# Sums over partitions with a matrix of ones: one fp32 product against two float32r products of split operands

## What is computed

```
def l2norm(x):
    return x * lax.rsqrt(jnp.sum(x * x, axis=-1, keepdims=True) + EPS)
...
q = l2norm(q.reshape(bsz, s, GDN_HEADS, GDN_DK).astype(f32)) * (GDN_DK ** -0.5)
k = l2norm(k.reshape(bsz, s, GDN_HEADS, GDN_DK).astype(f32))
g = -jnp.exp(gdn_a_log.astype(f32)) * jax.nn.softplus(gdn_a.astype(f32) + gdn_dt_bias.astype(f32))
...
gcum = jnp.cumsum(heads_to_chunks(g), axis=-1)
```

## Time and profile before

| | |
|---|---|
| median of 3 runs | 2578.36 us (2577.38 to 2578.86) |
| span of the profiled execution | 2574.7 us |
| TensorE (PE) busy | 2549.0 us, 99% |
| VectorE (DVE) busy | 1367.1 us, 53% |
| ScalarE (ACT) busy | 1237.7 us, 48% |
| GpSimd (POOL) busy | 79.9 us, 3% |
| mean granted TensorE clock | 0.997 |
| chain that ended last | PE 98%, ACT 1%, DVE 1% |

### The profile page before, as it was taken

The page is one execution under the profiler, slowest core; times in us unless marked ns, Lnnn a source line. Parts: engine busy times, 40 slices in busy tenths (PEclk is TensorE's granted clock), DMA queues, the critical chain, the costliest instruction groups (busy, mean ns, idle before and its releaser), DMA issues.

```text
span 2574.7 us, 33533 instructions
## 1 busy us (share of the span) xinstructions
PE 2549.0 (99%) x11883; PEld 2122.4 (82%) x11883; DVE 1367.1 (53%) x1473; ACT 1237.7 (48%) x1490; POOL 79.9 (3%) x119
## 2 busy tenths in 40 slices
PE   8999999999999999999999999999999999999998
PEld 7888888888888888888888888888788888888886
DVE  5444454554455456666665564465554444544444
ACT  5444444454445564747475544444544444444442
POOL 3000000000011000101010000000100000000000
PEclk9999999999999999999999999999999999999999
DMA  7666666656677654545454666665666666666654
GB/s 248 189 188 187 190 185 194 188 197 194 193 236 247 189 164 131 155 130 152 125 149 130 188 188 194 193 239 191 189 194 188 189 187 189 187 193 238 195 191 146
DMA packets 286022, 478.90 MB, mean 186 GB/s; under 512 B 17389, under 2 KB 91249, under 8 KB 285169
## 3 DMA queue, kind: packets, MB, share of 16 engines
q1 hardware_dynamic: 279648, 455.16, 58.8%
q0 software_dynamic: 5200, 20.50, 2.3%
q10 hardware_dynamic: 1088, 2.10, 0.3%
HBM read 469.30 MB, written 8.39 MB: 186 GB/s over the span
## 4 chain that ended last, share of the span: by engine, by line
PE 98%; ACT 1%; DVE 1%; DMA 0%; issue 0%; POOL 0%; POOLq 0%; DVEq 0%; ACTq 0%
PE acc L481 91%; PE mix L500 1%; PE mix L709 1%; PE mix L698 1%; PE mix L732 1%; PE mix L702 0%; PE mix L651 0%; DVE nat L1330 0%; PE mix L684 0%; PE mix L585 0%; PE mix L620 0%; DMA nat<-x 0%; ACT whi L869 0%; PE mix L665 0%; PE mix L664 0%
## 5 line engine op out<-in xcount | busy, mean ns | idle before, releaser
L1275 DVE TENSOR_TENSOR wlo<-raw,whi 128x1024 fp32r<-128x1024 f32 x860 | 1050.9, 1224 | 894.5 <-ACT whi L869 891.0
L869 ACT ACTIVATE whi<-raw 128x1024 fp32r<-128x1024 f32 x860 | 910.6, 1060 | 1240.8 <-PE acc L481 1213.7
L481 PE MATMUL acc<-whi,x_hi 128*128 128x512 f32 x1664 | 651.0, 391 | 0.3 <-DVE wlo L1662 0.3
L481 PE MATMUL acc<-whi,x_lo 128*128 128x512 f32 x1664 | 648.1, 389 | 0.0
L481 PE MATMUL acc<-wlo,x_hi 128*128 128x512 f32 x1664 | 647.6, 389 | 0.0
L481 PEld LDWEIGHTS acc<-whi,x_lo 128*128 128x128 f32 x1664 | 312.5, 188 | 65.3
L481 PEld LDWEIGHTS acc<-whi,x_hi 128*128 128x128 f32 x1664 | 312.8, 188 | 64.3 <-issue 0.7
L481 PEld LDWEIGHTS acc<-wlo,x_hi 128*128 128x128 f32 x1664 | 312.7, 188 | 63.9
L481 PE MATMUL acc<-whi,u_hi 128*128 128x512 f32 x896 | 361.7, 404 | 0.0
L481 PE MATMUL acc<-whi,u_lo 128*128 128x512 f32 x896 | 349.9, 390 | 0.0
L481 PE MATMUL acc<-wlo,u_hi 128*128 128x512 f32 x896 | 349.2, 390 | 0.0
(11 more groups left out here) (300 smaller groups left out, 1422.9 us busy)
## 6 DMA issues: line engine op xcount, KB each, us to landing
raw<-w_ffn_gu SPq DMA_DIRECT2D x352, 512.0 KB
raw<-w_ffn_down SPq DMA_DIRECT2D x176, 512.0 KB
raw<-w_in SPq DMA_DIRECT2D x224, 256.0 KB
raw<-w_in SPq DMA_DIRECT2D x96, 512.0 KB
raw<-w_mem_kv SPq DMA_DIRECT2D x32, 512.0 KB
raw<-w_out SPq DMA_DIRECT2D x32, 512.0 KB
raw<-w_in SPq DMA_DIRECT2D x64, 128.0 KB
raw<-w_up_gla SPq DMA_DIRECT2D x16, 512.0 KB
```

Source lines behind the costliest of these rows:

```text
L481: ins = nc.tensor.matmul(acc[:, par, t, :], x[:, k0 + k, cols], w[:, s, k, :], start=first and k == 0 and m == 0, stop=last and k == UK - ...
L869: act(whi[:, s], raw[:, s], ACT.Copy).then_inc(hi_ready, 1)
L1275: tt(wlo[:, s], raw[:, s], whi[:, s].bitcast(fp32), ALU.subtract).then_inc(lo_ready, 1)
```

## The change

Both sums with ones are made of float32r parts:

- A second matrix of ones, `onesr`, is set in float32r by POOL in the prologue.
- The log decays are split once, in `small_steps` (step 4 on DVE, three more small instructions); `st` grows from 5 to 7 rows and `gs` from 10 to 14, so that each group's constants hold the two parts.
- POOL makes two products, `zbh` and `zbl`, in place of one, before it signals `grhs_ready`. Step 1 on TensorE is two float32r products.
- In step 3 ACT waits for `gsums_done` before it squares (the new tiles lie over `sq`), then for its own square, and copies it to float32r (`sqh`, 128x1024) ahead of `zg` and `rg`.
- In step 4 DVE subtracts (`sql`, 128x1024, written over `sq`) and signals `sq_split`, ahead of its reduction. TensorE waits for `sq_split` and makes four float32r products in place of two in fp32.
- `STEP_AT` gets a slot without a step between steps 3 and 4 and loses the one between steps 25 and 26. Steps 4 to 25 are one slot later than before; steps 0 to 3, 26 and 27 stay in their slots. `TAKE_AT` follows step 22, from slot 26 to slot 27.
- 22 semaphores that are used once are folded into three (`once`); what waits for what stays the same.

```
-STEP_AT = ([0, 1, None, 2, 3, 4, 5, None] + list(range(6, 26)) + [None, 26, 27] + 32 * [None])
+STEP_AT = ([0, 1, None, 2, 3, None, 4, 5, None] + list(range(6, 28)) + 33 * [None])
...
+            [("zbh", U4, f32r), ("zbl", U4, f32r), ("gap", [P, 8, P], fp32), ("sqh", [P, 8, P], f32r)],
+            [("sql", [P, 8, P], f32r)],
...
-                pl.tensor_tensor(zb[:, :, :].rearrange("p (h t) n -> p h t n", t=NT),
-                                 tri[:, :].unsqueeze(1).unsqueeze(1).broadcast_to([P, 2, NT, P]),
-                                 gs[:, 0:NT, :].rearrange("p t h -> p h t").unsqueeze(3).broadcast_to([P, 2, NT, P]),
-                                 ALU.mult).then_inc(sem("grhs_ready"), 1)
+                for dst, o in ((zbh, 10), (zbl, 12)):
+                    ins = pl.tensor_tensor(dst[:, :, :].rearrange("p (h t) n -> p h t n", t=NT),
+                                           tri[:, :].unsqueeze(1).unsqueeze(1).broadcast_to([P, 2, NT, P]),
+                                           gs[:, o:o + NT, :].rearrange("p t h -> p h t").unsqueeze(3).broadcast_to([P, 2, NT, P]),
+                                           ALU.mult)
+                ins.then_inc(sem("grhs_ready"), 1)
...
-                    nc.tensor.matmul(mix[:, 3, :], ones[:, :], zb[:, :, :].rearrange("p u n -> p (u n)"),
-                                     start=True, stop=True).then_inc(sem("gsums_done"), 1)
+                    nc.tensor.matmul(mix[:, 3, :], onesr[:, :], zbh[:, :, :].rearrange("p u n -> p (u n)"), start=True, stop=False)
+                    nc.tensor.matmul(mix[:, 3, :], onesr[:, :], zbl[:, :, :].rearrange("p u n -> p (u n)"),
+                                     start=False, stop=True).then_inc(sem("gsums_done"), 1)
...
-                    need("sq_ready")
+                    need("sq_split")
                     for b in range(2):
-                        nc.tensor.matmul(mix[:, b, :], ones[:, :], sq[:, 4 * b:4 * b + 4, :].rearrange("p u n -> p (u n)"),
-                                         start=True, stop=True)
+                        for part, s in enumerate((sqh, sql)):
+                            nc.tensor.matmul(mix[:, b, :], onesr[:, :], s[:, 4 * b:4 * b + 4, :].rearrange("p u n -> p (u n)"),
+                                             start=part == 0, stop=part == 1)
...
+                    need("gsums_done")
                     act(sq[:, :, :], conv[:, 0:4, :].rearrange("p a (b n) -> p (a b) n", n=P), ACT.Square).then_inc(sem("sq_ready"), 1)
+                    need("sq_ready")
+                    act(sqh[:, :, :], sq[:, :, :], ACT.Copy).then_inc(sem("sq_hi"), 1)
                     act(zg[:, :, :], pr[:, 1, :, 256:512], ACT.Silu)
...
+                    ve.wait_ge(*once("logdecay"))
+                    nc.vector.tensor_copy(ghr[:, :, :], st[:, 0]).then_inc(once("g_hi")[0], 1)
+                    ve.wait_ge(*once("g_hi"))
+                    nc.vector.tensor_copy(st[:, 5], ghr[:, :, :].bitcast(fp32))
+                    tt(st[:, 6], st[:, 0], ghr[:, :, :].bitcast(fp32), ALU.subtract).then_inc(once("g_lo")[0], 1)
+                    ve.wait_ge(*once("g_lo"))
...
                 if j == 4:
 
+                    need("sq_hi")
+                    tt(sql[:, :, :], sq[:, :, :], sqh[:, :, :].bitcast(fp32), ALU.subtract).then_inc(sem("sq_split"), 1)
                     need("xa_scores")
```

More of the change, by code:

```diff
@@ L75 @@
 SPLIT_SMALL = 20
+ONCE = {"act_once": ("wsm_hi", "small_T_ready", "small_out", "tanh_b", "lrT_ready", "softplus", "exp_g", "exp_rest"),
+        "pe_once": ("small_done", "small_rows", "lrT_done", "gsum_done"),
+        "dve_once": ("wsm_lo", "beta", "a_bias", "softplus_sum", "logdecay", "g_hi", "g_lo", "g_out", "g_rest", "neg_beta")}
 LOG_SCALE = -0.5 * math.log(GDN_D)
@@ L114, in sem, with once @@
             return sems[name]
+        def once(name):
+            for of, names in ONCE.items():
+                if name in names:
+                    return sem(of), names.index(name) + 1
         raw = sb("raw", [P, RING, UK, CW])
@@ L144, in hybrid_layer @@
              ("mkh", [P, 2, SEQ], fp32), ("mvh", [P, 2, 256], fp32)],
+            [("zbh", U4, f32r), ("zbl", U4, f32r), ("gap", [P, 8, P], fp32), ("sqh", [P, 8, P], f32r)],
+            [("sql", [P, 8, P], f32r)],
             [("res_ffn2", [P, NT, D], fp32), ("post_ffn2", [P, D], fp32)])
+        zbh, zbl, sqh, sql = (ov[k] for k in ("zbh", "zbl", "sqh", "sql"))
         x_hi, x_lo = ov["x_hi"], ov["x_lo"]
@@ L175, in hybrid_layer @@
         ones = sb("ones", [P, P])
+        onesr = sb("onesr", [P, P], f32r)
+        ghr = sb("ghr", [P, NT, GDN_H], f32r)
         tri = sb("tri", [P, P])
@@ L188, in hybrid_layer @@
         dtb = sb("dtb", [P, GDN_H])
-        st = sb("st", [P, 5, NT, GDN_H])
+        st = sb("st", [P, 7, NT, GDN_H])
         stw = sb("stw", [P, 4, NT, GDN_H])
-        gs = sb("gs", [P, 10, 2])
+        gs = sb("gs", [P, 14, 2])
         cwg = sb("cwg", [P, TAPS * 3, 2])
@@ L350, in _ @@
             pl.dma_start(convn[:, :], a["gdn_conv"][0].rearrange("s (k p) -> (s k) p", p=P)).then_inc(sem("vecs_in"), 16)
+            const(pl.memset(onesr[:, :].bitcast(fp32), 1.0))
             const(pl.memset(tri[:, :], 1.0))
@@ L581, in small_steps @@
                 if j == 0:
-                    pe.wait_ge(sem("wsm_lo"), 1)
+                    pe.wait_ge(*once("wsm_lo"))
                     for k in range(KT_D):
@@ L586, in small_steps @@
                                                    start=k == 0 and m == 0, stop=k == KT_D - 1 and m == 2)
-                    ins.then_inc(sem("small_done"), 1)
+                    ins.then_inc(once("small_done")[0], 1)
                 if j == 1:
-                    pe.wait_ge(sem("small_T_ready"), 1)
+                    pe.wait_ge(*once("small_T_ready"))
                     for t in range(NT):
                         ins = nc.tensor.transpose(mix[:, 1, t * 32:(t + 1) * 32], small_T[:, t * P:(t + 1) * P], ident[0:32, 0:32])
-                    ins.then_inc(sem("small_rows"), 1)
+                    ins.then_inc(once("small_rows")[0], 1)
                 if j == 3:
-                    pe.wait_ge(sem("small_out"), 1)
+                    pe.wait_ge(*once("small_out"))
                     for t in range(NT):
                         ins = nc.tensor.transpose(mix[0:RANK, 1, t * P:(t + 1) * P], small[:, t, 0:RANK], ident)
-                    ins.then_inc(sem("lrT_done"), 1)
+                    ins.then_inc(once("lrT_done")[0], 1)
                 if j == 7:
-                    pe.wait_ge(sem("logdecay"), 1)
+                    pe.wait_ge(*once("logdecay"))
                     av = st[:, 0].rearrange("p t h -> p (t h)")
                     nc.tensor.matmul(mix[:, 2, 0:16], tri[:, :], av, start=True, stop=True)
-                    nc.tensor.matmul(mix[:, 2, 16:32], ones[:, :], av, start=True, stop=True).then_inc(sem("gsum_done"), 1)
+                    nc.tensor.matmul(mix[:, 2, 16:32], ones[:, :], av, start=True, stop=True).then_inc(once("gsum_done")[0], 1)
             def mixer_steps(slot, g):
@@ L991, in tasks @@
                         ac.wait_ge(sem("wsm_in"), 2 * 16)
-                        act(wsmh[:, :, :], wsm[:, :, :], ACT.Copy).then_inc(sem("wsm_hi"), 1)
+                        act(wsmh[:, :, :], wsm[:, :, :], ACT.Copy).then_inc(once("wsm_hi")[0], 1)
                     if j % U_D == U_D - 1:
@@ L1018, in small_steps @@
                 if j == 0:
-                    ac.wait_ge(sem("small_done"), 1)
-                    act(small_T[:, :], mix[0:32, 0, 0:SEQ], ACT.Copy).then_inc(sem("small_T_ready"), 1)
+                    ac.wait_ge(*once("small_done"))
+                    act(small_T[:, :], mix[0:32, 0, 0:SEQ], ACT.Copy).then_inc(once("small_T_ready")[0], 1)
                 if j == 2:
                     ac.wait_ge(sem("norm_rs"), R_H1 + 1)
-                    ac.wait_ge(sem("small_rows"), 1)
+                    ac.wait_ge(*once("small_rows"))
                     for t in range(NT):
                         ins = act(small[:, t, :], mix[:, 1, t * 32:(t + 1) * 32], ACT.Copy, scale=rs[:, R_H1, t:t + 1])
-                    ins.then_inc(sem("small_out"), 1)
-                    ac.wait_ge(sem("small_out"), 1)
-                    act(stw[:, 0], small[:, :, RANK:RANK + GDN_H], ACT.Tanh, scale=0.5).then_inc(sem("tanh_b"), 1)
+                    ins.then_inc(once("small_out")[0], 1)
+                    ac.wait_ge(*once("small_out"))
+                    act(stw[:, 0], small[:, :, RANK:RANK + GDN_H], ACT.Tanh, scale=0.5).then_inc(once("tanh_b")[0], 1)
                 if j == 3:
-                    ac.wait_ge(sem("lrT_done"), 1)
-                    act(lrT[:, :], mix[0:RANK, 1, 0:SEQ], ACT.Copy).then_inc(sem("lrT_ready"), 1)
-                    ac.wait_ge(sem("a_bias"), 1)
+                    ac.wait_ge(*once("lrT_done"))
+                    act(lrT[:, :], mix[0:RANK, 1, 0:SEQ], ACT.Copy).then_inc(once("lrT_ready")[0], 1)
```

(37 more changed lines are left out.)

## The result

The changed kernel takes 2602.44 us (median of 4 runs, 2601.65 to 2603.57); the kernel before took 2577.87 beside it. The ratio is 1.0094, with a 95% interval from 1.0082 to 1.0106: 24.6 us slower. The forecast was 2595.3 with a range from 2586 to 2604. The profiled execution has a span of 2600.0 us against 2574.7.

What follows compares the result with a forecast made beforehand. TensorE, 98% of the last-ending chain, was taken as the bound. Per group -1.23 (products) + 4.15 (wait) + 1.30 (tail) = +4.22, +16.9 over four groups: 2578.4 + 16.9 = 2595.3 us, range 2586 to 2604.

Steps and rivals of the forecast that it cites:

- The gain: TensorE's sums in steps 1 and 4: float32r products at 0.227 us each save 0.41 and 0.82, 1.23 us a group.
- The wait for `sql`: At step 4 TensorE waits 4.34 us for `sql` behind ACT's and DVE's queues, 4.15 a group more than before.
- the two readings of POOL's part: Before `sql`, POOL's `rg` takes its turn (wait 4.34 us, chosen, 0.35), or `sql` follows DVE's split at once (3.16, chance 0.27).
- The tail: Steps 26 and 27: TensorE late by 1.30 us a group, as the chain of step 25 moves one unit later.
- The take-out: ACT's take-out in slot 15 now meets step 12, where ACT has nothing; claimed to cost nothing.
- POOL's second product: Before step 1: ends at 1062.1, ahead of TensorE at 1063.54, so no cost; uncovered at most 1.03 a group.
- the ring: Loads by SP that wait for late DVE splits: claimed to have more than a ring's turn, so no cost.
- the small instructions: Prologue's memset and three DVE instructions of `small_steps`, once only: taken as 0, 0 to 1.6 us in all.
- the likeliest case: Longer wait at step 4, no fall of the clock: +4.22 a group, +16.9 in all, 2595.3 us; chance 0.35.
- the 2.7 us into the wait: Clock fell there in TensorE's 5.3 us wait outside the mixer; the clock case was said to decide from such a wait.
- this rival: Clock falls behind each new TensorE wait, 2.1 us a group, +8.4: 2603.7 with the longer wait; chance 0.20.
- 3.7 us: Distance by which the median of runs stands above the profiled span, added to turn span 2591.6 into 2595.3.

Runs made afterwards that it cites:

- e5: Changed kernel with one DVE instruction, `sql`, moved from step 4 (slot 6) to the start of slot 5, ahead of DVE's split; ratio 0.9995 to the kernel before.
- e6: Changed kernel with `sql` ahead of DVE's split, steps 26 and 27 one slot later, POOL's decay products ahead of its DMAs; 2572.08 us, ratio 0.9975.
- e3: Changed kernel with only `STEP_AT` put back to the line of before; 2588.66 us against 2578.54 for the kernel before, ratio 1.0037.
- e1: Kernel before with only the table `STEP_AT` of the changed kernel; 2582.35 us against 2578.54, ratio 1.0017.
- e2: Changed kernel with the old table and the squares summed in fp32 again, so only the decay sums are split; ratio 0.9992 to the kernel before.
- e4: Changed kernel with one more wait on POOL: its `zg` and `rg` products start only when `sql` is done; ratio 1.0065 to the kernel before.
- e7: Changed kernel with ACT's SiLUs of `zg` and `rg` moved from step 3 to the start of its step 4; ratio 1.0028 to the kernel before.
- e8: Changed kernel with steps 26 and 27 one slot later and POOL's decay products ahead of its DMAs, `sql` left behind the split; ratio 1.0083.

## Why the prediction was right, and what it missed

**The gain.** The step that priced the products at -1.23 held: 0.23 us between starts in step 1, where before it was 0.86 for the one product; in step 4 of e5 (957.56 on), where nothing waits, all four products start 0.22 to 0.23 apart. e6, which has the gain without the waits, takes 1.34 off a group, of 1.42.

**The wait for `sql`.** The chain through ACT's `zg` and `rg`, its split and DVE's split gave 4.34 us; the trace has 4.25. Of the two readings of POOL's part the one chosen was right: `sql` took 2.28, and 1.22 with POOL held back. e5 shows that it is the place in DVE's queue, and e3 that the added slot makes it longer.

**The tail.** 1.30 forecast, 1.30 in e1. In the changed kernel it is the same: from step 24 at 1048.97 to step 27 at 1060.29 are 11.32 us against 10.01, so 1.31. The take-out, POOL's second product, the ring and the small instructions cost nothing, as was said; e2 and e5 show no wait for them.

**The clock is what was missed.** The likeliest case was given without a fall of the clock and with a total of +16.9; measured are +24.6. The step that failed stands under the rivals: "Against it: most of the observed fall lay in a wait longer than mine, and it need not meet all four." It met all four in the profiled executions of the change, of e4 and of e3, at waits booked at 4.1, 2.8 and 2.4 us alike, and none at 1.8 (e7). The first half of the sentence misreads its own rows as well: of the fall before, 2.6 us lay in the wait and at least 4.2 behind it. The rival's total, 2603.7, is the closest of all the cases; its price was 2.1 a group and 1.71 was measured. The wrong use of the rows was to take the 2.7 us into the wait at which the clock fell before for a limit: in e3 it fell 0.3 to 0.7 us after the wait, which was shorter than that. The range held because it had been drawn up to this rival, which got a chance of 0.20; the likeliest case alone was 7 us short, on a change of 24.6.

The Trainium skill, "TensorE: Matmul & The Clock Gate", section "Why this matters for your kernels", warns against idle gaps between bursts of products, as throughput drops behind them, and so spoke for this rival. The trace agrees with it, at 0.50 behind each of the four waits; the waits of e3 and e4 are shorter than the gaps that the page warns of, and the clock fell at them all the same.

The Trainium skill, "SBUF — State Buffer", section "SBUF: two separate sides", has the port pair that VectorE and GpSimd share as an exclusive lock, held for a whole instruction. The traces agree, with `sql` at 2.28 beside POOL and 1.22 without. That the engine which waits gets the lock ahead of the next instruction of the one that holds it was my reading of the earlier trace rows; the page leaves it open.

**The way from span to median.** The forecast adds 3.7 us, the distance between the profiled span of before and the median. That is not only what lies around a span: a run's time stands 2.0 us above its own span before and 1.6 in the changed kernel. The rest is that the profiled execution of before was an early one: its span is 2574.7, and other executions of that kernel have up to 2578.6. The two parts of the sum that this joins, +16.9 and the median of before, do not hang on it.

## What to carry to other kernels

Before cheaper arithmetic on the critical engine is paid for with work on idle engines, follow the new operand through every queue on its way: what counts is not its duration but what stands ahead of it in each queue, and an added slot can put one more piece there. A gap of some 2.4 us in TensorE's stream here cost 1.7 us more through the clock in each of four groups, so such a wait is priced nearly twice; at 1.8 us five of six runs seem free of that price. Where only the place is wrong, moving is enough: with the same arithmetic, one instruction moved (e5) turned +0.94% into -0.05%, and the table and POOL's order with it (e6) into -0.25%.

## What the runs showed that was not expected

- The clock's fall need not lie in the wait: it came 2.1 us before its end (e8), 0.3 us behind it (the changed kernel, 961.72 against 961.39) and up to 1.4 us behind it (e4). It then stayed down for 3.4 us wherever it fell behind the mixer's wait or up to 0.4 us ahead of the wait's end, and for 6.8 where it fell 0.75 us or more ahead (e8). At the wait outside the mixer it stayed down for 6.8 us in both kernels, in the changed one though it fell only 0.3 us ahead of the end.
- VectorE and GpSimd took turns instruction by instruction: DVE's split got in between POOL's two products, and POOL's second got in between DVE's split and `sql`, though neither engine's own next instruction had anything else to wait for.
